# Moving the buffer of the low weight halves to another byte offset in a matmul-bound decoder step

## The reference

```python
def decoder_layer(x, pos, ret_S0, rwkv_S0, shift0, p):
    x = x + 0.5 * swiglu(rms_norm(x, p['norm_ffn1']), p['ffn1_w_gu'], p['ffn1_w_down'])
    h = rms_norm(x, p['norm_mix'])
    z = h @ p['w_in']
    zq, zk, zv, zg, zs, zgr, zgw = jnp.split(z, Z_SPLITS, axis=-1)
    ret_S, o_ret = retention_branch(zq, zk, zv, zg, pos, ret_S0)
    rwkv_S, o_rwkv, shift = rwkv7_branch(zs, shift0, rwkv_S0, p)
    merged = (jax.nn.sigmoid(zgr) * (o_ret @ p['w_ret_o'])
              + jax.nn.sigmoid(zgw) * (o_rwkv @ p['w_rwkv_o']))
    x = x + merged @ p['w_out']
    x = x + 0.5 * swiglu(rms_norm(x, p['norm_ffn2']), p['ffn2_w_gu'], p['ffn2_w_down'])
    return x, ret_S, rwkv_S, shift
```

## Time and profile before

| | |
|---|---|
| median of 3 runs | 2866.72 us (2866.03 to 2868.74) |
| profiled execution | 2868.76 us, span 2867.0 us |
| mean granted TensorE clock | 0.997 |
| PE busy | 2841.1 us (99%) |
| PEld busy | 2768.5 us (97%) |
| DVE busy | 1564.2 us (55%) |
| ACT busy | 1117.0 us (39%) |
| POOL busy | 107.2 us (4%) |
| 16 DMA engines | 173 GB/s mean |

### The profile page before, as it was taken

One profiled execution on the slowest core, in us unless ns is written; L12 is line 12 of the kernel. 1 busy time (PEld: TensorE's weight loads), 2 busy tenths in 40 slices (PEclk: granted clock), 3 DMA queues, 4 the chain that ended last, 5 costly groups with the idle time before them and its releaser, 6 DMA issues.

```text
span 2867.0 us, 57289 instructions
## 1 busy us (share of the span) xinstructions
PE 2841.1 (99%) x24662; PEld 2768.5 (97%) x24662; DVE 1564.2 (55%) x1679; ACT 1117.0 (39%) x1121; POOL 107.2 (4%) x144
## 2 busy tenths in 40 slices
PE   9999999999999999999999999999999999999998
PEld 8999999999999999898998999999999999999998
DVE  6444444444567576775865555466544444454454
ACT  5333333333344453544534644233433333333333
POOL 0000000000000002011020010000000000000000
PEclk9999999999999999999999999999999999999999
DMA  5444454444456553635436444555444445444454
GB/s 205 167 163 164 162 171 176 161 171 155 164 186 228 190 186 111 249 131 200 162 139 240 176 154 165 187 203 184 164 172 161 166 161 171 175 162 167 155 169 144
DMA packets 85460, 495.80 MB, mean 173 GB/s; under 512 B 10320, under 2 KB 10496, under 8 KB 44096
## 3 DMA queue, kind: packets, MB, share of 16 engines
q1 hardware_dynamic: 71424, 444.14, 44.0%
q0 software_dynamic: 9280, 32.72, 3.1%
q10 hardware_dynamic: 4608, 16.78, 1.5%
HBM read 462.80 MB, written 30.80 MB: 172 GB/s over the span
## 4 chain that ended last, share of the span: by engine, by line
PE 93%; DVE 3%; ACT 2%; DMA 1%; issue 0%; SPq 0%; ACTq 0%; DVEq 0%; POOLq 0%
PE psum L545 29%; PE psum L546 29%; PE psum L547 29%; PE psum L893 1%; PE psum L709 1%; DVE sb_w_lo L1506 1%; DMA sb_raw<-in_w_wo 0%; DMA sb_raw<-in_gu 0%; PE psum L666 0%; ACT sb_w_hi L1094 0%; DVE sb_w_lo L1512 0%; ACT sb_w_hi L1085 0%; PE psum L906 0%; PE psum L903 0%; PE psum L745 0%
## 5 line engine op out<-in xcount | busy, mean ns | idle before, releaser
L547 PE MATMUL psum<-sb_h,sb_w_lo 128*128 128x288 f32 x4384 | 1297.7, 296 | 0.0
L546 PE MATMUL psum<-sb_h,sb_w_hi 128*128 128x288 f32 x4384 | 1293.9, 295 | 0.0
L545 PE MATMUL psum<-sb_h,sb_w_hi 128*128 128x288 f32 x4384 | 1288.5, 294 | 4.2 <-DVE sb_w_lo L1506 1.7
L1512 DVE TENSOR_TENSOR sb_w_lo<-sb_raw,sb_w_hi 128x2048 fp32r<-128x2048 f32 (+1 forms) x348 | 712.4, 2047 | 713.8 <-ACT sb_w_hi L1085 713.2
L1085 ACT ACTIVATE sb_w_hi<-sb_raw 128x2048 fp32r<-128x2048 f32 (+1 forms) x349 | 600.2, 1720 | 1207.6 <-PE psum L547 1177.5
L545 PEld LDWEIGHTS psum<-sb_h,sb_w_hi 128*128 128x128 f32 x4384 | 828.4, 189 | 28.5 <-issue 19.9
L547 PEld LDWEIGHTS psum<-sb_h,sb_w_lo 128*128 128x128 f32 x4384 | 823.9, 188 | 0.0
L546 PEld LDWEIGHTS psum<-sb_h,sb_w_hi 128*128 128x128 f32 x4384 | 821.5, 187 | 1.3 <-issue 1.0
L547 PE MATMUL psum<-sb_g,sb_w_lo 128*128 128x288 f32 x1408 | 416.8, 296 | 0.0
L546 PE MATMUL psum<-sb_g,sb_w_hi 128*128 128x288 f32 x1408 | 415.4, 295 | 0.0
L545 PE MATMUL psum<-sb_g,sb_w_hi 128*128 128x288 f32 x1408 | 407.0, 289 | 0.0
(11 more groups left out here) (380 smaller groups left out, 2389.0 us busy)
## 6 DMA issues: line engine op xcount, KB each, us to landing
sb_raw<-in_gu SPq DMA_DIRECT2D x175, 1024.0 KB, 4.8
sb_raw<-in_down SPq DMA_DIRECT2D x128, 704.0 KB, 4.1
sb_raw<-in_w_mix SPq DMA_DIRECT2D x72, 1024.0 KB, 4.9
sb_raw<-in_w_gates SPq DMA_DIRECT2D x32, 1024.0 KB, 5.4
sb_s_ret<-in_s_ret POOLq DMA_DIRECT2D x32, 512.0 KB, 8.4
out_ret_s<-sb_s_ret ACTq DMA_DIRECT2D x32, 512.0 KB, 5.4
sb_raw<-in_w_ro SPq DMA_DIRECT2D x16, 1024.0 KB, 4.8
sb_raw<-in_w_out SPq DMA_DIRECT2D x16, 1024.0 KB, 4.8
```

The costliest lines, as they stand in the source:

```text
L545: pe.matmul(out, wh, xh, start=start, stop=False)
L546: pe.matmul(out, wh, xl, start=False, stop=False)
L547: return pe.matmul(out, wl, xh, start=False, stop=stop)
L1512: dve.tensor_tensor(w_lo[:, slot, 0:cols], raw[:, slot, 0:cols], w_hi[:, slot, 0:cols].bitcast(F32), ALU.subtract).then_inc(lo_made, 2)
```

## The change

The buffer of the low weights begins at 48 instead of 128 from the high weights, modulo 256. As `sb` works in multiples of 32 bytes, the counter is aligned to 32 and the buffer gets 16 bytes (4 elements) more, which `w_lo` skips. The small tiles `own` and `gains` are allocated at other places in the order: `eps_c` stays where it was, `own` moves behind `w_lo` (from offset 32 to 64), `gains` moves ahead of `mean_w`, `head_w` and `ident`. These four keep their offsets modulo 256, as 256 bytes of `gains` change sides. All tiles from `arena` on, and `h`, stay at the byte where they were. No instruction is added, removed or reordered on any engine.

```diff
-LINES, APART = 256, 144
+LINES, APART, LOW_APART = 256, 144, 48
...
         w_hi = sb("w_hi", [P, 2, BLK], F32R)
-        eps_c = sb("eps_c", [P, 3])
-        first_root = eps_c[:, 2:3]
-        own = sb("own", [P, SB])
 
         def align(apart):
...
-        align(4 * T % LINES)
-        w_lo = sb("w_lo", [P, 2, BLK], F32R)
+        eps_c = sb("eps_c", [P, 3])
+        first_root = eps_c[:, 2:3]
+        align(LOW_APART)
+        w_lo = sb("w_lo", [P, LOW_APART % 32 // 4 + 2 * BLK], F32R)
+        w_lo = w_lo[:, LOW_APART % 32 // 4:].rearrange("p (slot c) -> p slot c", slot=2)
+        own = sb("own", [P, SB])
         h_hi, h_lo = halves_of("h", KT)
+        gains = sb("gains", [P, 4, KT])
         mean_w = sb("mean_w", [P, P])
         head_w = sb("head_w", [P, P], F32R)
         ident = sb("ident", [P, P])
-        gains = sb("gains", [P, 4, KT])
         arena = place[0]
```

## The result

| | before | after |
|---|---|---|
| median | 2866.38 us (2863.68 to 2871.5, 12 runs) | 2853.35 us (2830.77 to 2876.58, 12 runs) |
| ratio, 95% interval | | 0.9927 [0.9897, 0.9956] |
| profiled execution | 2868.76 us, span 2867.0 us | 2833.03 us, span 2831.2 us |

One run of the changed kernel, 2876.58 us, is over 1.5% above its fastest and is left out of the ratio; no trace of it was kept, so what slowed it is open. The kernel is faster by 0.7% in the ratio and by 0.5% in the median (13.0 of 2866.38 us). Both hide that its executions come in groups: five lie within 2830.77 to 2833.86 us, five within 2852.99 to 2859.66, one at 2863.94. The kernel before has no such groups. The profile shows one of the fastest.

A forecast was written before the change was run, and what follows sets the result against it. PE's throughput was taken to bound the kernel. 6560 triples each losing 3.1 ns in the second gap gave 20.3 us less, all else at nothing: median 2846.4 us from 2866.72, range 2815 to 2886.

The forecast's parts named there:

- PE's throughput bounds, each ns of a triple is 6.6 us: Whole kernel: PE busy 2841.1 of 2867.0 us; 6560 triples (three matmuls each) of 0.3934 us make 90% of the span.
- Small tiles and VectorE's write at nothing: Moved own and gains, and DVE's writing of w_lo (2.29 us per 2048 columns, slack 2.0 us): costed at 0.
- The second gap loses 3.1 ns, the first and third keep their length: Between matmul starts in a triple: 131.7 ns, where low weights load, falls to about 128.6; 126.7 and 135.0 stay.
- the sign that the delay is carried from one matmul to the next: In feed-forward: if the first gap, where no low weights are read, moves from 126.7 ns, the split by gaps is wrong.
- The cost shrinks in proportion to the step between loads: PE's weight loads: offset step 48 instead of 128 leaves 0.375 of the second gap's 5.0 ns excess, 3.1 ns less.
- The sum of 20.3 us and the median of 2846.4: Whole kernel: 6560 triples times 3.1 ns saved, taking the median from 2866.72 to 2846.4 us (-0.7%).
- the forecast's own range of 2834 to 2858: Whole kernel: time in us if only the second gap shrinks, by some 1 to 5 ns; chance 0.44.
- my rival of both gaps: Second and third gaps of each triple both shrink: 8.3 ns per triple, 54.5 us, 2812 us; chance 0.17.
- Rival of no change, with the rule of two independent read ports: PE's loads of low weights: placement does not matter, as loading takes no bandwidth from the running matmul; 2866.7 us, chance 0.16.
- Rival of closeness: Low load 32 bytes from the low activation stream instead of 112 slows each triple 3.3 ns: +21.5 us, 2888 us; chance 0.23.
- my upper end of 4.9: Triples could lengthen by 4.9 ns, as the retention output projection's 398.3 ns exceeds other stages: +32 us if all cost it.
- the prediction's estimate of 360 for streaming: Per triple: each matmul's 288 columns take 120 ns at 2.4 GHz, leaving 33.4 ns as something else, 219 us in all.

The follow-up runs named there:

- The pair of kernels with mixed offsets: Low weights written at 128, mostly read at 48, from the kernel before: 2843.36 us; written at 48, mostly read at 128, from the changed kernel: 2885.78 us.
- the locked stretch: Changed kernel run again unaltered, 2855.01 us; in its profile one feed-forward half of 1056 triples ran at 406.7 ns each.
- small tiles alone: Kernel before with only own and gains placed as in the change, low weights still at 128: 2867.17 us against 2867.45, ratio 0.9998.

## Why the prediction came out as it did

- *PE's throughput bounds, each ns of a triple is 6.6 us.* Right. 6.7 ns in feed-forward gave 14.1 us per feed-forward, and the clock and the other engines' busy times stayed, while waits for low weights went from 3.8 to 4.5 us.
- *Small tiles and VectorE's write at nothing.* Right, both by experiment: ratio 0.9998 for the tiles, 2292 ns for the write, and the gain followed the read.
- *The second gap loses 3.1 ns, the first and third keep their length.* The second gap did lose 3.3 ns and stands at 128.4, where the prediction named 128.6. The step that failed is counting this gap alone: the third lost 7.5 and the first grew by 4.1, together another 3.4 ns, so that a triple lost 6.7 and not 3.1. The growth of the first is what I had named as the sign that the delay is carried from one matmul to the next. The pair of kernels with mixed offsets, and the locked stretch, show that it is. A triple is a pattern as a whole, often several triples are, and its time can't be split by gaps. So the hit in the second gap confirms nothing.
- *The cost shrinks in proportion to the step between loads.* Wrong, not only in size. At a step of 0 the kernel is 1.3% slower than before, and its second gap is 134.5 ns where the proportion gives 126.7. The inference rested on one pair of gaps with equal offsets and unequal length; that pair shows that history matters, and I read a distance into it.
- *The sum of 20.3 us and the median of 2846.4.* The measured gain in the median is 13.0 us, the ratio is 0.7% below 1 as forecast, and the forecast's own range of 2834 to 2858 holds the median. That is luck. Of the twelve executions none lies within 6 us of 2846.4: five are about 33 us below the kernel before, six are 2 to 13 us below it, one is above it, and median and ratio depend on how many fell into each group. The profiled one is 35.7 us faster, between my forecast and my rival of both gaps, whose 8.3 ns per triple was nearer to the 6.7 measured, though it too kept the first gap fixed.
- *Rival of no change, with the rule of two independent read ports.* The time did change, so the rival is wrong. The Trainium skill's page "TensorE: Matmul & The Clock Gate", Part 2 (What happens when you issue a matmul), has the load of the next weights take no read bandwidth from the running matmul. Here the starts move from 386.7 to 400.0 ns per triple with the address from which the low weights are loaded. So what the prediction drew from the rule, a sum of 0, does not follow. Whether it is bandwidth that is lost, or something else in the reading, no run here tells.
- *Rival of closeness.* Wrong as a rule (96 is slow, 48 fast), though its direction was right at 0, 16 and 32. Its price of 3.3 ns was too small, and so was my upper end of 4.9: 6.7 ns above before occurs.

## What to carry to other kernels

Where PE is busy all the time, read the starts of matmuls and not its busy share: here 33 ns of every 393 were above the prediction's estimate of 360 for streaming, and a byte offset moved the triple by 13 ns. Such an effect can't be interpolated from one placement or guessed from a distance, so try the offsets in steps of 16 bytes, each with one profile, and compare the count of matmuls in the same window. (Here eight offsets from 0 to 128 were tried; 48 is the best of these, and those at 112 and above 128 were not.) Look at means over hundreds of triples before reading a single gap: six triples gave 130 ns where a thousand give 128.4. Then look at all executions and not only the median: a placement can have a good and a bad steady pattern, and in the one case traced, which one a stretch got was settled at its first matmuls after a wait.

## What the runs showed of the hardware

- The time of three matmuls of 288 columns with a load each depends on the byte offset of the loaded low weights in SBUF, at one clock: 386.7, 393.3, 397.6 to 398.6 and 400.0 ns. No run moved the buffer by a whole 256 bytes, so the modulus is not shown directly; what speaks for it is that within a stretch the distance between stream and load changes from triple to triple by multiples of 256, and the pattern of gaps does not.
- Where every triple of a stretch is alike, it took 386.7, 393.3, 400.0 or 406.7 ns, in steps of 6.7 ns, which is 16 periods of the 2.4 GHz clock. Where 2, 3, 5 or 8 triples make a cycle, the cycle's sum is a multiple of the same 6.67 ns. Why is open.
- One triple loaded from another offset than its neighbours changed the two or three triples behind it, to 400 and 407 ns, more than the common pattern of either offset (386.7 and 393.3).
- The same program at the same place in two executions ran 1056 triples at 386.7 and at 406.7 ns, and kept to each until PE was next made to wait. With the low weights at 128, the two profiles (before, and small tiles alone) show 393.3 ns in the window of feed-forward 1.
